# Prompt attention of a decoder step: turning of weights three units behind the scores in place of two

## The chip, the cores and the metric

One Trainium2 chip, one of its cores. The metric is the device time of one execution in microseconds (us). The kernel is written by hand for each engine: TensorE (PE, its weight loads PEld), VectorE (DVE), ScalarE (ACT), GpSimd (POOL) and SyncE (SP, which only starts DMAs), each with its own queue of instructions that it works off in order, and semaphores between them.

## What is computed

One step of a one-layer hybrid decoder: a prompt of 1024 tokens and 64 sample tokens, model width 1024. RMSNorm, one projection into queries, keys and values of 16 heads of width 64, attention, RMSNorm, output projection, residual, RMSNorm, an MLP with squared ReLU, final RMSNorm. Eight heads use stick-breaking attention, eight use dilated window attention with a softmax. For the prompt, cut to what matters here:

```python
# stick-breaking, strictly causal
z = q @ k.T * d**-0.5 + sb_bias[h]
log_1m = where(mask, log_sigmoid(-z), 0.0)
excl = cumsum(log_1m, reverse=True) - log_1m
o = where(mask, exp(log_sigmoid(z) + excl), 0.0) @ v
# dilated: the three patterns (128,1), (512,4), (2048,16), mixed by their softmax denominators
logits = q @ k.T * d**-0.5 + rel_bias[bucket(distance)]
```

The kernel joins the three dilated patterns to one softmax over all keys: a table by distance holds the bias plus the logarithm of how many patterns take that distance.

## The kernel before, in words

The stages run one after another: first norm, projection with sample attention, a stage that writes keys and values in natural order, **prompt attention** (prompt_stage, L924), output projection (dense_stage), MLP, store. Only prompt_stage is touched by the diff.

prompt_stage works through NU = 64 units. A unit is one pair of heads (two heads at once, 64 rows of TensorE each), one kind (stick-breaking, SB, or dilated, DIL) and one block of 128 queries. Query block q needs q + 1 blocks of 128 keys. For each of the four pairs come eight SB units and then eight DIL units. The list `order` (L933) takes the query blocks as 0, 7, 1, 6, 2, 5, 3, 4, so that the units of each eight are 1, 8, 2, 7, 3, 6, 4, 5 key blocks wide. In this document A0 to A7 are the eight SB units of a pair in this order, D0 to D7 its eight DIL units; so A1 and D1 have eight blocks, A3 and D3 seven. Light units (1, 2, 3, 4 blocks) have one piece, heavy ones (8, 7, 6, 5) have two: a piece is at most PW = 512 keys, four blocks. Light and heavy units alternate.

What is done for a unit:

- score (L1060, on PE): q times k for both heads into s_ps, two slots of one piece each; for SB the last block also gets a causal mask (L1081). It waits until the piece two before has been read out (L1072).
- SB: gate (L1130, ACT): two sigmoids per head and piece, into take (L1145) and stay (L1147). stay has two slots, so the gates of an SB unit wait for the product of the SB unit two before (L1134). Then broken (L1190, DVE): a reverse running product over stay for each head (L1197), times take in place (L1201).
- DIL: dilated (L1203, DVE): scale and bias for each piece into take (L1215), then the row minimum (L1221). Then exponent (L1151, ACT): exp over the unit, once per head, in place in take (L1157).
- turn (L1084, PE): 128 by 128 transposes of take into t_ps (L1095). t_ps has two slots of one piece of one head. So a unit with two pieces fills both slots with its first piece (head 0, head 1), and the second piece waits until ACT has copied them (L1093).
- copy_out (L1160, ACT): t_ps into wtsT (L1169), in SBUF.
- values (L1098, PE): v times the turned weights into o_ps (L1107), for DIL also ones times the weights for the softmax sum (L1112). It waits for o_out of the unit two before.
- o_out (L1223, DVE): a copy for SB (L1230), a reciprocal and a product for DIL (L1235, L1237), into o_T. SP stores o_T once eight units of a kind are done (L1042).

Each engine has one loop over a step s, and the order in it is the order of its queue. On PE (L1116): score(s) piece 0, turn(s-2) piece 0, score(s) piece 1, turn(s-2) piece 1, values(s-3). On ACT (L1172): gate(s) piece 0, copy_out(s-2) piece 0, gate(s) piece 1, copy_out(s-2) piece 1, and last exponent(s). On DVE (L1239): dilated(s), broken(s-1), o_out(s-4). The step is named by the unit that is scored in it, so that "step D3" is the one that scores D3.

take has WS = 4 slots of one unit (both heads, 1024 keys). Whoever writes a slot (gate L1136, dilated L1211) waits until the unit that held it, s-4, has been turned.

Of the rest, POOL turns the DIL queries around, once a pair (L1053), and SP loads q, k and v of the pair after next (L1008).

Of the kernel before, what the change touches and what calls it, by code (L numbers as in the profile page):

```python
# [382 lines left out]
def dense_stage(nc, cx, tag, weights, src, gain, ones, groups, hi, lo, turns, load=None, store=None, residual=None, keep=None,  # L383
# [10 lines left out]

    PW = 256
    per = KC // groups
    with ExitStack() as st:
# [16 lines left out]
        with nc.Block() as block:  # L414
            @block.sync
            def _(sp):
                def fetch(i, s):
                    col = i * 2 * PW + s * PW
                    col = col if isinstance(i, int) else sp.snap(col)
# [504 lines left out]
def prompt_stage(nc, cx, qkvT, oT, by_distance, sb_bias, neg_causal, ident, ones, v_nat):  # L924
# [3 lines left out]

    SB, DIL = 0, 1
    NU = 2 * PAIRS * QT  # L930
    WS = 4
    PW = 512
    order = [q for i in range(QT // 2) for q in (i, QT - 1 - i)]  # L933

    def unit(s):
# [3 lines left out]
    def kind(s):  # L939
        return s // QT % 2  # L940

    def width(s):
        return (unit(s)[2] + 1) * P

    def pieces(s):
        return [(a, min(PW, width(s) - a)) for a in range(0, width(s), PW)]

# [18 lines left out]
    with ExitStack() as st:  # L966
# [7 lines left out]
        stay = sb("stay", [P, 2, 2, SEQ])  # L974
        take = sb("take", [P, WS, 2, SEQ])
        prod = sb("prod", [P, 2, SEQ + 1])
# [29 lines left out]
        with nc.Block() as block:  # L1006
# [49 lines left out]
            @block.tensor  # L1056
            def _(pe):
                pe.wait_ge(tables_ready, 4)

                def score(s, some):  # L1060
                    j, k, q = unit(s)
                    if s % QT == 0:
                        pe.wait_ge(qk_loaded[k][j % 2], 32 * (j // 2 + 1))
                        if k == DIL:
                            pe.wait_ge(q_turned, j + 1)
                    for p, (a, n) in enumerate(pieces(s)):
                        if p not in some:
                            continue
                        g = piece[s, p]
                        if g >= 2:  # L1070
                            k2, count = scores_read[g - 2]
                            pe.wait_ge((gates, logits)[k2], count)  # L1072
                        masked = k == SB and a + n == width(s)
                        for h in range(2):
                            rows, cols = slice(h * HD, (h + 1) * HD), slice(q * P, (q + 1) * P)
                            queries = q_back[rows, j % 2, cols] if k == DIL else q_in[rows, SB, j % 2, cols]
                            last = pe.matmul(s_ps[:, g % 2, h, 0:n], queries, k_in[rows, k, j % 2, a:a + n], start=True,
                                             stop=not masked)
                        if masked:
                            for h in range(2):  # L1080
                                last = pe.matmul(s_ps[:, g % 2, h, n - P:n], identb[:, :], maskb[:, :], start=False, stop=True)  # L1081
                        last.then_inc(scored, 1)

                def turn(s, some):  # L1084
                    j, k, q = unit(s)
                    pe.wait_ge((sb_weights, dil_weights)[k], (1, 2)[k] * (of_kind(s, k) + 1))
                    for p, (a, n) in enumerate(pieces(s)):
                        if p not in some:
                            continue
                        for h in range(2):  # L1090
                            g = turned_piece[s, p, h]
                            if g >= 2:
                                pe.wait_ge(copied, g - 1)  # L1093
                            for b in range(0, n, P):
                                last = pe.transpose(t_ps[:, g % 2, b:b + P], take[:, s % WS, h, a + b:a + b + P], ident[:, :])  # L1095
                            last.then_inc(turned, 1)

                def values(s):  # L1098
                    j, k, q = unit(s)
                    pe.wait_ge(copied, 2 * pieces_to(s + 1))  # L1100
                    if s >= 2:
                        pe.wait_ge(o_copied, s - 1)
                    if s % QT == 0:
                        pe.wait_ge(v_loaded[k][j % 2], 16 * (j // 2 + 1))
                    for c in range(q + 1):
                        for h in range(2):
                            last = pe.matmul(o_ps[h * HD:(h + 1) * HD, s % 2, 0:P], v_in[:, k, j % 2, c, h * HD:(h + 1) * HD],  # L1107
                                             wtsT[:, s % 2, h, c, :], start=(c == 0), stop=(c == q))
                    if k == DIL:
                        for c in range(q + 1):  # L1110
                            for h in range(2):
                                last = pe.matmul(o_ps[h * HD:(h + 1) * HD, s % 2, P:2 * P], ones[:, 0:HD],  # L1112
                                                 wtsT[:, s % 2, h, c, :], start=(c == 0), stop=(c == q))
                    last.then_inc(o_done, 1)

                for s in range(NU + 3):  # L1116

                    for p in range(2):
                        if s < NU:
                            score(s, [p])  # L1120
                        if 0 <= s - 2 < NU:
                            turn(s - 2, [p])
                    if 0 <= s - 3 < NU:
                        values(s - 3)

            @block.scalar
            def _(act):
                act.wait_ge(tables_ready, 4)

                def gate(s, some):  # L1130
                    j, k, q = unit(s)
                    w = of_kind(s, SB)
                    if w >= 2:
                        act.wait_ge(sb_weights, w - 1)  # L1134
                    if s >= WS:
                        act.wait_ge(turned, 2 * pieces_to(s - WS + 1))  # L1136
                    for p, (a, n) in enumerate(pieces(s)):
                        if p not in some:
                            continue
                        g = piece[s, p]  # L1140
                        act.wait_ge(scored, g + 1)
                        for h in range(2):
                            head = 2 * j + h
                            z = s_ps[:, g % 2, h, 0:n]
                            act.activation(take[:, s % WS, h, a:a + n], z, ACT.Sigmoid, scale=SCALE,  # L1145
                                           bias=zb[:, 0, head:head + 1])
                            last = act.activation(stay[:, w % 2, h, a:a + n], z, ACT.Sigmoid, scale=-SCALE,  # L1147
                                                  bias=zb[:, 1, head:head + 1])
                        last.then_inc(gates, 1)

                def exponent(s):  # L1151
                    r = of_kind(s, DIL)
                    act.wait_ge(topped, r + 1)
                    for h in range(2):

                        x = take[:, s % WS, h, 0:width(s)]
                        act.activation(x, x, ACT.Exp, bias=top[:, r % 2, h:h + 1], scale=-1.0)\  # L1157
                           .then_inc(dil_weights, 1)

                def copy_out(s, some):  # L1160
                    if s >= 2:
                        act.wait_ge(o_done, s - 1)
                    for p, (a, n) in enumerate(pieces(s)):
                        if p not in some:
                            continue
                        for h in range(2):
                            g = turned_piece[s, p, h]
                            act.wait_ge(turned, g + 1)
                            act.activation(wtsT[:, s % 2, h, a // P:(a + n) // P, :], t_ps[:, g % 2, 0:n].rearrange(  # L1169
                                "p (c q) -> p c q", q=P), ACT.Copy).then_inc(copied, 1)  # L1170

                for s in range(NU + 3):  # L1172
                    for p in range(2):
                        if s < NU and kind(s) == SB:
                            gate(s, [p])
                        if 0 <= s - 2 < NU:
                            copy_out(s - 2, [p])
                    if s < NU and kind(s) == DIL:
                        exponent(s)

            @block.vector
            def _(dve):
# [53 lines left out]
                    dve.wait_ge(inverted, r + 1)  # L1236
                    dve.tensor_tensor(out, o[:, ::-1], one_over[:, ::-1], ALU.mult).then_inc(o_copied, 1)  # L1237

                for s in range(NU + 4):  # L1239
                    if s < NU and kind(s) == DIL:  # L1240
                        dilated(s)
                    if 0 <= s - 1 < NU and kind(s - 1) == SB:
                        broken(s - 1)
                    if 0 <= s - 4 < NU:
                        o_out(s - 4)


def projection_and_sample_stage(nc, cx, w_in, hi, lo, root, qkvT, oT, sb_bias, sb_caches, win_caches, q_back, new_rows, neg_new,
# [786 lines left out]
```

## Time and profile before

| | |
|---|---|
| median of 3 runs | 2104.06 us (2103.48 to 2105.66) |
| the profiled execution | 2106.2 us, its span 2104.4 us |
| PE busy | 1795.7 us, 85% of the span |
| DVE busy | 941.0 us, 45% |
| ACT busy | 560.9 us, 27% |
| POOL busy | 522.3 us, 25% |
| mean granted TensorE clock | 0.928 of full speed |

The span is from the first to the last instruction in the profile of one execution. Prompt attention lies between about 797 and 1141 us of it. Times in rows are us from the start of the span, durations in us.

### The profile page before, as it was taken

The page shows a single profiled execution, that of the slowest core. Times are in us where ns is not written, and L with a number is a line of the kernel's source. Part 1 is how long each engine was busy: PE and PEld are TensorE (multiplying, and loading weights), DVE is VectorE, ACT ScalarE, POOL GpSimd, SP SyncE. Part 2 cuts the span into 40 slices and gives each one's busy share as a digit, 9 for nine tenths or more (in the row PEclk, how much of TensorE's full clock was granted, in tenths as well). Part 3 has the DMA queues.
Part 4 walks back from the last instruction along what each step waited for, and adds up shares of the span by engine and source line. Part 5 has one row for each costly group of instructions (what it writes and reads, how often), then busy time and mean ns, then how long its engine had stood idle before and what let it go on. Part 6 is the DMA issues. An engine that isn't in the chain of part 4 may idle for free. (4 is left out here: it accounts for less than half of the span.)

```text
span 2104.4 us, 39226 instructions
## 1 busy us (share of the span) xinstructions
PE 1795.7 (85%) x17442; PEld 1554.3 (74%) x17442; DVE 941.0 (45%) x858; ACT 560.9 (27%) x927; POOL 522.3 (25%) x391
## 2 busy tenths in 40 slices
PE   6659579988789955978976696999999999999997
PEld 4447467766667743655644696999999999999997
DVE  2237347747457225787875847312121222122123
ACT  2202112202122115666664303202121111112022
POOL 0133436654466400000001113111122211122210
PEclk7889789998799967999998798999999999999999
DMA  7758779988799785121002403243333434333422
GB/s 208 262 201 335 268 275 390 414 351 325 279 343 414 278 320 202 41 81 41 12 11 113 158 1 127 93 167 123 131 119 119 157 122 139 119 119 119 160 99 95
DMA packets 112774, 385.74 MB, mean 183 GB/s; under 512 B 15064, under 2 KB 44248, under 8 KB 100568
## 3 DMA queue, kind: packets, MB, share of 16 engines
q0 software_dynamic: 39936, 251.41, 31.8%
q1 hardware_dynamic: 65912, 129.77, 17.6%
q10 hardware_dynamic: 6800, 2.68, 0.6%
q8 instruction: 102, 1.67, 0.3%
q14 instruction: 24, 0.20, 0.0%
HBM read 348.64 MB, written 102.04 MB: 214 GB/s over the span
## 5 line engine op out<-in xcount | busy, mean ns | idle before, releaser
L637 POOL TENSOR_TENSOR mlp_w_lo<-mlp_raw,mlp_w_hi 128x2048 fp32r<-128x2048 f32 x30 | 138.1, 4604 | 586.0 <-ACT mlp_w_hi L683 586.0
L1789 DVE STREAM_TRANSPOSE sa_kT<-sa_k_in 128x2048 f32<-128x2048 f32 x64 | 144.2, 2290 | 141.3 <-PE sa_s L1518 140.8
L796 DVE TENSOR_TENSOR xT<-xT,mlp_acc 128x1088 f32<-128x1088 f32 x64 | 82.5, 1289 | 278.7 <-PE mlp_acc L378 278.7
L378 PE MATMUL mlp_acc<-n_hi,mlp_w_hi 128*128 128x272 f32 x1024 | 171.8, 290 | 21.2 <-POOL mlp_w_lo L354 16.3
L1509 PE MATMUL sa_acc<-n_hi,sa_wh 128*128 128x512 f32 x384 | 158.5, 413 | 22.2 <-POOL sa_wl L1444 22.2
L378 PE MATMUL mlp_acc<-mlp_h_hi,mlp_w_hi 128*128 128x272 f32 x1024 | 170.4, 288 | 4.0 <-DVE mlp_h_lo L792 4.0
L378 PE MATMUL mlp_acc<-n_lo,mlp_w_hi 128*128 128x272 f32 x1024 | 170.7, 289 | 0.0
L378 PE MATMUL mlp_acc<-n_hi,mlp_w_lo 128*128 128x272 f32 x1024 | 170.5, 289 | 0.0
L378 PE MATMUL mlp_acc<-mlp_h_lo,mlp_w_hi 128*128 128x272 f32 x1024 | 169.6, 288 | 0.0
L378 PE MATMUL mlp_acc<-mlp_h_hi,mlp_w_lo 128*128 128x272 f32 x1024 | 169.6, 287 | 0.0
L378 PEld LDWEIGHTS mlp_acc<-n_hi,mlp_w_hi 128*128 128x128 f32 x1024 | 145.3, 190 | 22.5 <-POOL mlp_w_lo L354 16.5
L1595 PE MATMUL sa_o<-sa_v_in,sa_wtsT 128*16 128x128 f32 x2688 | 98.7, 290 | 65.9 <-DMA sa_v_in<-in_cache_win_v,sa_w_rows 32.7
L1509 PE MATMUL sa_acc<-n_lo,sa_wh 128*128 128x512 f32 x384 | 153.5, 400 | 0.0
L1509 PE MATMUL sa_acc<-n_hi,sa_wl 128*128 128x512 f32 x384 | 153.2, 399 | 0.0
L789 DVE SCALAR_TENSOR_TENSOR mlp_h<-mlp_acc,mlp_root 128x1088 f32<-128x1088 f32 x32 | 41.3, 1291 | 238.5 <-PE mlp_acc L378 238.1
L378 PEld LDWEIGHTS mlp_acc<-mlp_h_hi,mlp_w_hi 128*128 128x128 f32 x1024 | 143.6, 188 | 5.7 <-DVE mlp_h_lo L792 5.7
L378 PEld LDWEIGHTS mlp_acc<-n_lo,mlp_w_hi 128*128 128x128 f32 x1024 | 145.0, 189 | 0.0
L378 PEld LDWEIGHTS mlp_acc<-n_hi,mlp_w_lo 128*128 128x128 f32 x1024 | 144.7, 189 | 0.0
L378 PEld LDWEIGHTS mlp_acc<-mlp_h_lo,mlp_w_hi 128*128 128x128 f32 x1024 | 143.7, 188 | 0.0
L378 PEld LDWEIGHTS mlp_acc<-mlp_h_hi,mlp_w_lo 128*128 128x128 f32 x1024 | 143.7, 188 | 0.0
L1471 POOL DMA_INDIRECT sa_v_in<-in_cache_sb_v,v_rows x128 | 122.9, 960 | 76.4 <-PE sa_o L1595 51.6
L1595 PEld LDWEIGHTS sa_o<-sa_v_in,sa_wtsT 128*16 128x16 f32 x2688 | 68.1, 100 | 97.3 <-DMA sa_v_in<-in_cache_sb_v,v_rows 44.7
(180 smaller groups left out, 3006.5 us busy)
## 6 DMA issues: line engine op xcount, KB each, us to landing
out<-in_cache_win_k POOLq DMA_DIRECT2D x16, 2040.0 KB, 8.6
out<-in_cache_win_v POOLq DMA_DIRECT2D x16, 2040.0 KB, 8.6
mlp_raw<-in_w_up SPq DMA_DIRECT2D x16, 1024.0 KB, 11.7
mlp_raw<-in_w_down SPq DMA_DIRECT2D x16, 1024.0 KB, 11.3
fi_w<-in_w_in SPq DMA_DIRECT2D x24, 512.0 KB, 9.2
sa_wr<-in_w_in SPq DMA_DIRECT2D x24, 512.0 KB
qkvT<-sa_out SPq DMA_DIRECT2D x48, 256.0 KB, 5.5
na_rows_in<-qkvT SPq DMA_DIRECT2D x16, 512.0 KB, 7.0
```

What stands on the lines that cost most here:

```text
L378: last = pe.matmul(out[:, b, 0:BW], w[:, k, w_cols], x[:, k, b * BW:(b + 1) * BW], start=(k == 0 and part == 0), stop=(k == kn - 1 and par ...
L637: pool.tensor_tensor(out=ring.lo[:, n % 2, :], in0=ring.raw[:, n % 2, :], in1=ring.hi[:, n % 2, :].bitcast(F32), op=ALU.subtract).then_inc ...
L789: dve.scalar_tensor_tensor(out=in_banks(act_h[:, c % 2, :]), in0=acc[:, c % 2, :, 0:BW], scalar=0.0, in1=in_banks(root[:, :]), op0=ALU.max ...
L796: dve.tensor_tensor(in_banks(xT[:, c, :]), in_banks(xT[:, c, :]), acc[:, c % 2, :, 0:BW], ALU.add).then_inc(added, 1)
L1471: pool.indirect_dma_start(v_in[:, y % VS, :], None, src, bass.IndirectOffsetOnAxis(ap=rows, axis=0)).then_inc(v_loaded[y % VS], 16)
L1509: last_one = pe.matmul(acc[:, z % 3, :], w[:, k, :], x[:, k, cols], start=(k == 0 and part == 0), stop=(k == KC - 1 and part == 2))
L1595: last_one = pe.matmul(o_ps[c * 32:c * 32 + 2 * TS, a, :], w[:, a, c * 2 * TS:(c + 1) * 2 * TS], v[:, c * P:(c + 1) * P], start=False, sto ...
L1789: dve.transpose(kT[:, x % KT, :, :].rearrange("p x (j k) -> p j x k", k=32), k_in[:, x % KS, :, :].rearrange("p j (x d) -> p j x d", d=32) ...
```

## The change

Three constants or offsets change: the turning stands LAG = 3 steps behind the scores in place of 2, and with it copy_out, values and o_out one step later each; take has five slots in place of four. Gates, exponents, running products and their order among themselves stay as they are. take grows by 8 KB in each partition.

```diff
-    WS = 4
+    WS = 5
     PW = 512
+    LAG = 3
...
-                for s in range(NU + 3):
+                for s in range(NU + LAG + 1):
 
                     for p in range(2):
                         if s < NU:
                             score(s, [p])
-                        if 0 <= s - 2 < NU:
-                            turn(s - 2, [p])
-                    if 0 <= s - 3 < NU:
-                        values(s - 3)
+                        if 0 <= s - LAG < NU:
+                            turn(s - LAG, [p])
+                    if 0 <= s - LAG - 1 < NU:
+                        values(s - LAG - 1)
...
-                for s in range(NU + 3):
+                for s in range(NU + LAG + 1):
                     for p in range(2):
                         if s < NU and kind(s) == SB:
                             gate(s, [p])
-                        if 0 <= s - 2 < NU:
-                            copy_out(s - 2, [p])
+                        if 0 <= s - LAG < NU:
+                            copy_out(s - LAG, [p])
                     if s < NU and kind(s) == DIL:
                         exponent(s)
...
-                for s in range(NU + 4):
+                for s in range(NU + LAG + 2):
...
-                    if 0 <= s - 4 < NU:
-                        o_out(s - 4)
+                    if 0 <= s - LAG - 2 < NU:
+                        o_out(s - LAG - 2)
```

## Rows read from the trace of the kernel before

**Rows 1.** Windows: one A and one D stretch; busy us of PE, PEld, DVE, ACT, POOL.

```profile
966.30:1009.00 42.70, 33.54 (x300) 21.47 (x296) 32.90 (x33) 31.65 (x69) 1.13 (x1) 0.96 0.15 50
...
1009.00:1049.80 40.80, 38.00 (x394) 26.83 (x394) 32.12 (x37) 25.02 (x47) 0.00 (x0) 0.96 0.04 15
```

**Rows 2.** Timeline of DVE: running products of A6, the four pairs.

```profile
835.94 2.33 DVE L1197 TENSOR_TENSOR_SCAN pr_prod<-pr_stay 128x512 f32<-128x512 f32 x2
...
918.82 2.33 DVE L1197 TENSOR_TENSOR_SCAN pr_prod<-pr_stay 128x512 f32<-128x512 f32 x2
...
1002.85 2.33 DVE L1197 TENSOR_TENSOR_SCAN pr_prod<-pr_stay 128x512 f32<-128x512 f32 x2
...
1086.03 2.33 DVE L1197 TENSOR_TENSOR_SCAN pr_prod<-pr_stay 128x512 f32<-128x512 f32 x2
```

**Rows 3.** List of waits in the stage: us in total, times, longest us.

```profile
PE pr_turned L1095 <- DVE pr_take L1201: 28.1, 16, 5.3
```

**Rows 4.** Timeline of ACT and DVE, A stretch: gates, copies, running products.

```profile
815.16 1.10 ACT L1169 ACTIVATE pr_wtsT<-pr_turned 128x512 f32<-128x512 f32 x2
...
816.82 0.58 ACT L1145 ACTIVATE pr_take<-pr_scores,pr_zb 128x384 f32<-128x384 f32 x1 [0.55 <-PE pr_scores L1081]
...
818.84 3.94 DVE L1197 TENSOR_TENSOR_SCAN pr_prod<-pr_stay 128x896 f32<-128x896 f32 x2 [3.95 <-ACT pr_stay L1147]
...
821.49 0.73 ACT L1169 ACTIVATE pr_wtsT<-pr_turned 128x256 f32<-128x256 f32 x2
...
830.62 3.41 DVE L1197 TENSOR_TENSOR_SCAN pr_prod<-pr_stay 128x768 f32<-128x768 f32 x2 [2.02 <-ACT pr_stay L1147]
...
973.51 0.52 ACT L1169 ACTIVATE pr_wtsT<-pr_turned 128x128 f32<-128x128 f32 x2
...
984.37 0.58 ACT L1145 ACTIVATE pr_take<-pr_scores,pr_zb 128x384 f32<-128x384 f32 x1 [0.20 <-PE pr_scores L1081]
```

**Rows 5.** Timeline, third pair, from D0 to D3.

```profile
1008.21 0.42 DVE L1215 SCALAR_TENSOR_TENSOR pr_take<-pr_scores,pr_bias 128x256 f32<-128x256 f32 x1 [1.57 <-PE pr_scores L1077]
...
1009.00 2.86 DVE L1197 TENSOR_TENSOR_SCAN pr_prod<-pr_stay 128x640 f32<-128x640 f32 x2
...
1017.38 2.29 DVE L1221 TENSOR_REDUCE pr_top<-pr_take 128x2 f32<-128x2048 f32 x1
...
1019.70 2.19 ACT L1157 ACTIVATE pr_take<-pr_take,pr_top 128x1024 f32<-128x1024 f32 x2 [2.67 <-DVE pr_top L1221]
...
1022.50 1.22 DVE L1215 SCALAR_TENSOR_TENSOR pr_take<-pr_scores,pr_bias 128x1024 f32<-128x1024 f32 x1 [1.12 <-PE pr_scores L1077]
```

**Rows 6.** Timeline of PE, ACT and DVE, third pair, from step D6 to the fourth A1.

```profile
1037.95 1.75 PE L1107 MATMUL pr_o<-pr_wtsT,pr_v_in 128*64 128x128 f32 x28 [0.17 <-DVE pr_o_T L1237]
...
1045.19 0.82 PE L1112 MATMUL pr_o<-pr_wtsT,ones 128*64 128x128 f32 x12
...
1045.76 1.55 ACT L1157 ACTIVATE pr_take<-pr_take,pr_top 128x640 f32<-128x640 f32 x2 [0.79 <-DVE pr_top L1221]
...
1045.94 0.49 PE L1077 MATMUL pr_scores<-pr_k_in,pr_q_in 64*128 64x128 f32 x4
...
1051.49 0.69 ACT L1145 ACTIVATE pr_take<-pr_scores,pr_zb 128x512 f32<-128x512 f32 x1 [0.76 <-PE pr_scores L1077]
...
1057.23 4.47 DVE L1197 TENSOR_TENSOR_SCAN pr_prod<-pr_stay 128x1024 f32<-128x1024 f32 x2 [5.04 <-ACT pr_stay L1147]
```

**Rows 7.** TensorE after two idle gaps of like length, and a window.

```profile
896.87 1.09 PE L1095 MATMUL pr_turned<-ident,pr_take 128*128 128x128 f32 x8 [2.45 <-DVE pr_take L1201]
...
980.58 1.76 PE L1095 MATMUL pr_turned<-ident,pr_take 128*128 128x128 f32 x8 [2.45 <-DVE pr_take L1201]
...
981.00:985.00 4.00, 4.00 (x21) 2.54 (x19) 3.93 (x6) 3.80 (x8) 1.13 (x1) 0.59 0.51 162
```

**Rows 8.** Timeline of DVE, end of the stage.

```profile
1126.04 1.22 DVE L1215 SCALAR_TENSOR_TENSOR pr_take<-pr_scores,pr_bias 128x1024 f32<-128x1024 f32 x1 [1.02 <-PE pr_scores L1077]
...
1140.83 0.29 DVE L1237 TENSOR_TENSOR pr_o_T<-pr_o,pr_one_over 128x128 f32<-128x128 f32 x1
```

Columns of Rows 1, and of the last line of Rows 7: stretch, its length, busy us and instructions of PE, PEld, DVE, ACT and POOL, granted TensorE clock as a share of full speed, DMA share, GB/s. Columns of a timeline: start, duration of the merged instructions, engine, line, operation, output and inputs, shapes, count; in brackets the idle time of the engine before them and who ended it.

## The prediction

> **What bounds it now.** I read the windows by stretch first, then the timeline of the three engines over one whole pair, and the list of waits of the stage. Prompt attention takes some 344 us of the span of 2104.4; everything outside is the same code. In an A stretch no engine is full: of 42.70 us PE works 33.54, DVE 32.90, ACT 31.65; in a D stretch PE works 38.00 of 40.80 [rows 1]. So an A stretch is set by waits from engine to engine, and a D stretch nearly by PE's queue. The pairs repeat: from the running product of one A6 to the next it is 82.9, 84.0 and 83.2 us [rows 2], mean 83.4. The ring in an A stretch is stay, which has two slots and keeps them: product of A1, gates of A3, running product of A3, product of A3, gates of A5. PE waits in it too, 28.1 us over the stage for products that it is to turn [rows 3]; that wait the change takes away, but ACT and DVE stand in the ring without it. The fifth slot of take loosens nothing there. It only keeps the old slack: a slot has to be free one unit later, and is turned one step later.
>
> The point to see is the parity. Heavy and light units alternate, so two behind pairs heavy with heavy (score of A3 with turn of A1), three behind pairs heavy with light (score of A3 with turn of A0). That evens out PE's and ACT's work by step, and it takes something away: with LAG 2 a second piece of score stands between the two pieces of a heavy turn; with LAG 3 the two pieces follow each other, and the second needs ACT's copies of the first (t_ps has two slots).
>
> **Terms.** I carried each wait forward over one pair, with durations of equal shapes, and compare the marks with the rows.
>
> (a) A stretches, a gain. ACT's order for A3 is gates of piece 0, a copy, gates of piece 1. The copy was four blocks (1.10 us) and then 0.55 us of waiting for scores in the first pair, 0.20 in the third; it becomes one block (0.52), the scores long there [rows 4]. A3's running product starts 1.2 to 1.3 us earlier in the first pair; in later pairs, where the second wait is shorter, some 0.8. For A5 the copy of four blocks (1.10) becomes one of two (0.73) [rows 4], 0.5 with the short wait behind it. DVE, which has A2 and A4 to finish meanwhile, is free just before. First pair: -1.8 us; later ones -1.3 each.
>
> (b) D0 to D3, a gain that is lost again. Before, DVE waits 1.57 us for D0's score, which stands behind a held-up turn of A5 and the values of A4 [rows 5]. With LAG 3 PE has a light turn in step A7 and scores D0 as soon as A7's first gates are out. Third pair: the running product of A7 moves from 1009.00 to 1007.5, and, as both scores of D1 are then ready, the minimum of D1 from 1017.38 to 1014.5: 2.9 us ahead. But in step D2 PE must turn A7, whose second piece waits for ACT's copies of the first. ACT has them in its step D2, behind exponent(D1), which needs that minimum (2.29) and takes 2.1: until 1018.9. PE, done with the first piece at 1015.45, stands until 1019.5, four us; then come the rest of the turn and the values of A6 (1.0), and the first score of D3 starts at 1021.3. DVE reads it at 1022.45, against 1022.50 [rows 5]. Gain: nothing. This wait is new; behind it in PE's queue are values(A6) and score(D3), and DVE, with D2 done, waits for that.
>
> (c) D4 to D7. The same once more: turn(D1)'s second piece waits for copies behind exponent(D3), PE standing from 1026.5 to 1029.4; in D6 only 0.3. PE reaches A0 at 1046.6, against 1045.94; exponent(D7), which hangs on DVE, starts at 1045.5, against 1045.76 [rows 6]: -0.3. PE arrives a little late although it has the turn of D5 and the values of D4 still ahead.
>
> (d) D to A, a loss. In step A0 PE now turns D5, two pieces. The copies of the first stand behind exponent(D7), the table load and the gates of A0, until 1050.0 and 1050.6. Then come the second piece (to 1050.9) and the values of D4 (twelve matmuls for the sum 0.82 [rows 6], the values themselves as many, 1.5 together), and only then the first score of A1 (1.1). Its gates start at 1053.5, against 1051.49, and ACT's own work until the running product of A1 is unchanged, 5.74: 1059.3, against 1057.23 [rows 6]: 2.1 later, 2.3 counted from exponent(D7).
>
> (e) One pair, from A6 to A6: -0.3 + 2.3 - 1.3 = +0.7. Three times: +2.1. The last D stretch: -0.5 (its D0 waits longer than in the third pair).
>
> (f) The tail. When the last D7 is scored, PE has the turn of D4 (0.8) and the values of D3 (28 matmuls at 1.75 and as many for ones [rows 6], 3.3) still to do which it had behind it before. Nothing of later units hides them. From D7's first read-out to the last o_out it was 15.1 us [rows 8]; I get 19.1: +4.0. The next stage waits for this store, so it passes whole.
>
> (g) Without cost: SP's stores and loads stand a step later, but the loads run a whole pair ahead (tens of us); POOL waits for scores alone. Semaphores and instructions are the same in number. Were that cover gone, a store would count only at the end, where it counts now.
>
> Sum at the clock as it was: -1.8 + 2.1 - 0.5 + 4.0 = +3.8 us.
>
> (h) The clock. After 2.45 us of idle PE the eight transposes took 1.76 us at 980.58 and the stretch behind them had a granted clock of 0.59, mostly the lower level of 1.2 GHz; after the same 2.45 us at 896.87 they took 1.09, at 2.4 GHz [rows 7]. So a gap of that length is followed by the lower level sometimes. The new gaps of (b) and (c) are 4.1 and 2.9 us, eight in all, and behind each stands work on the path (values, then a score). Below: no new fall, 0. Above: all eight, each 1.4 us (0.7 for the eight transposes as in the row, and, an estimate, as much again for the score behind them, which takes about as long), 11. I take 4, three of eight, since one of the two gaps in the rows was followed by it. The Trainium skill, "TensorE: Matmul & The Clock Gate", section "HAM oscillation — how this bites in real kernels", says that a gap which recurs in every iteration can let the clock fall in each, so that every burst starts slow; by it the sum would go to its upper bound. The rows agree only in part: the same gap was once followed by a fall and once not.
>
> **Sum:** +3.8 + 4 = +8. The sum is made against one execution (2106.2 us, span 2104.4, 2.1 above the median); against the median: 2104.06 + 8 = 2112.
>
> **Rivals.** A measurement of this kernel can tell about 0.2%, 4.2 us.
> - The clock does not change: +3.8, 2107.9. For: the clock was at 0.96 of full speed in both stretches, with idle gaps in them [rows 1], and total idle PE time hardly grows. Against: the gaps are longer. 0.22.
> - Nothing net: waits are absorbed in slack, tail and start cancel apart from 2 us: 2104 to 2106. For: errors of 0.3 us in each of some ten marks could do it. 0.11. With it belongs that the change does not do what it says, because turning never waits for its weights in that step; against it stands the wait for products [rows 3].
> - Faster: the lead of (b) is kept. It decides in step D2: if PE comes to D3's first score before 1018.5 in place of 1021.3. Then each pair keeps 2.9: per pair +0.7 - 2.9 = -2.2, three times -6.6; start -1.8; last D stretch -0.5 - 2.9; tail +4.0: -7.8, 2096.3. For: DVE does get ahead. Against: ACT's queue has the copies behind exponent(D1), in order. 0.07.
> - Worse: all gaps are followed by the lower level, and gaps in the A stretches (PE in steps A4 and A6, some 2.8 us each) too: +3.8 + 11 + 2 = +17, 2121. 0.10.
>
> **Numbers.** Forecast (2108.3 to 2117): 0.50. Slower by over 0.2%: 0.50 + 0.10 + a fifth of the first rival, 0.05 = 0.65. Within: 0.17 + 0.11 = 0.28. Faster: 0.07. The range takes in the second rival's upper half and most of the worse one: 2105 to 2119. The likeliest case's own range is 2108 to 2117.
>
> **What would show it.** In the third pair, counted from A6's running product: D1's minimum near +11.6 (was 14.5), D3's first read-out near +19.6 (was 19.65), the running product of A1 near +56.5 (was 54.4), the next A6 near +84. Waits of PE's turn (L1095) for ACT's copy (L1169) should grow to some 15 us a pair, and those for products [rows 3] nearly go. Tail: 19 us from D7's read-out to the last o_out. Wrong if a pair takes under 83 us, or if PE does not stand in steps D2 and A0; if the pair takes 84 but the granted clock in the D stretches stays at 0.96 or more, (h) is wrong.

## The result and the profile after

The changed kernel takes 2133.07 us (median of 4, 2129.26 to 2134.84), the kernel before 2103.77 (median of 4): ratio 1.0138, 95% interval 1.0118 to 1.0159, so 25 to 33 us slower. The forecast was slower by 8, with a range to 2119. The profiled execution took 2129.26 us. The page of it opens:

```profile
span 2127.4 us, 39219 instructions
...
PE 1808.6 (85%) x17442; PEld 1559.2 (73%) x17442; DVE 939.2 (44%) x858; ACT 563.8 (27%) x927; POOL 524.4 (25%) x391
```

All of it lies in prompt attention. Its windows, as in [rows 1] (columns: stretch, length, busy us of PE, PEld, DVE, ACT, POOL, granted clock, DMA share, GB/s), here a D and an A stretch of the third pair and then the stage as a whole:

```profile
1016.00:1062.00 46.00, 38.79 (x370) 26.43 (x367) 31.28 (x35) 25.06 (x49) 0.00 (x0) 0.93 0.03 13
...
1062.00:1107.00 45.00, 35.51 (x345) 24.01 (x342) 32.67 (x34) 33.03 (x69) 0.00 (x0) 0.96 0.03 13
...
799.00:1164.00 365.00, 296.79 (x2746) 197.80 (x2742) 257.40 (x271) 228.12 (x453) 7.90 (x4) 0.91 0.14 49
```

The same for the stage of the kernel before:

```profile
800.00:1141.00 341.00, 284.51 (x2746) 193.14 (x2742) 259.41 (x272) 224.87 (x453) 5.46 (x4) 0.96 0.15 53
```

The work did not grow: DVE and ACT are busy as before. PE is busy 12 us longer with the same 2746 recorded matmuls, at a granted clock of 0.91 in place of 0.96; the other half of the 24 us is idle time. The running products of A6, the marks of [rows 2]:

```profile
833.69 2.33 DVE L1198 TENSOR_TENSOR_SCAN pr_prod<-pr_stay 128x512 f32<-128x512 f32 x2
...
922.64 2.33 DVE L1198 TENSOR_TENSOR_SCAN pr_prod<-pr_stay 128x512 f32<-128x512 f32 x2
...
1012.02 2.33 DVE L1198 TENSOR_TENSOR_SCAN pr_prod<-pr_stay 128x512 f32<-128x512 f32 x2
...
1103.42 2.33 DVE L1198 TENSOR_TENSOR_SCAN pr_prod<-pr_stay 128x512 f32<-128x512 f32 x2
```

A pair takes 89.0, 89.4 and 91.4 us, mean 89.9; it was 83.4, and +0.7 was forecast, before the clock. From the last A6 to the end of the stage it is longer too. The first load of the next stage, on SP's queue, after and before:

```profile
1167.46 0.38 SPq L423 DMA_DIRECT2D out_raw<-in_w_out  x1
```

```profile
1144.24 0.38 SPq L423 DMA_DIRECT2D out_raw<-in_w_out  x1
```

From the last A6 to this load it is 64.0 us, against 58.2. The list of waits of the stage (total us, times, longest); PE's wait for products [rows 3] is gone, and in its place stand these:

```profile
PE pr_turned L1096 <- ACT pr_wtsT L1170: 56.5, 32, 3.7
...
DVE pr_take L1216 <- PE pr_scores L1078: 53.7, 23, 6.1
```

Steps D2 to D4 of the third pair, on the timeline:

```profile
1027.90 2.19 ACT L1158 ACTIVATE pr_take<-pr_take,pr_top 128x1024 f32<-128x1024 f32 x2 [4.26 <-DVE pr_top L1222]
...
1029.99 1.76 ACT L1170 ACTIVATE pr_wtsT<-pr_turned 128x512 f32<-128x512 f32 x4
...
1030.71 0.73 PE L1096 MATMUL pr_turned<-ident,pr_take 128*128 128x128 f32 x2 [3.64 <-ACT pr_wtsT L1170]
...
1032.77 2.08 PE L1078 MATMUL pr_scores<-pr_k_in,pr_q_back 64*128 64x512 f32 x4
...
1034.96 1.22 DVE L1216 SCALAR_TENSOR_TENSOR pr_take<-pr_scores,pr_bias 128x1024 f32<-128x1024 f32 x1 [5.45 <-PE pr_scores L1078]
...
1042.07 1.85 PE L1096 MATMUL pr_turned<-ident,pr_take 128*128 128x128 f32 x8 [2.64 <-ACT pr_wtsT L1170]
...
1044.90 1.45 PE L1078 MATMUL pr_scores<-pr_k_in,pr_q_back 64*128 64x512 f32 x4
...
1046.47 1.84 DVE L1216 SCALAR_TENSOR_TENSOR pr_take<-pr_scores,pr_bias 128x1024 f32<-128x1024 f32 x2 [4.85 <-PE pr_scores L1078]
```

This is the chain of the forecast. ACT's exponent of D1 (1027.90, 2.19 us) stands ahead of its copies (1029.99). PE has turned the first piece of A7 and waits 3.64 us for the slots. But then the first score piece of D3 (four matmuls of 512 keys) takes 2.08 us and not 1.13, and DVE has waited 5.45 us for it; [rows 5] has 1.12 there. Two steps later once more: transposes 1.85, score 1.45, DVE 4.85 us idle. In this pair the same stands at two more places, which have no price in the forecast's sum. First the gap of step A6, and D0's read-out that it holds back:

```profile
1009.97 0.94 PE L1096 MATMUL pr_turned<-ident,pr_take 128*128 128x128 f32 x6 [2.29 <-ACT pr_wtsT L1170]
...
1011.43 2.08 PE L1078 MATMUL pr_scores<-pr_k_in,pr_q_in 64*128 64x512 f32 x4
...
1017.84 0.42 DVE L1216 SCALAR_TENSOR_TENSOR pr_take<-pr_scores,pr_bias 128x256 f32<-128x256 f32 x1 [2.02 <-PE pr_scores L1078]
```

Then step A0, up to the running product of A1:

```profile
1064.97 0.83 PE L1096 MATMUL pr_turned<-ident,pr_take 128*128 128x128 f32 x4 [2.29 <-ACT pr_wtsT L1170]
...
1068.21 1.74 PE L1078 MATMUL pr_scores<-pr_k_in,pr_q_in 64*128 64x512 f32 x4
...
1070.38 0.69 ACT L1146 ACTIVATE pr_take<-pr_scores,pr_zb 128x512 f32<-128x512 f32 x1 [4.15 <-PE pr_scores L1078]
...
1076.11 4.47 DVE L1198 TENSOR_TENSOR_SCAN pr_prod<-pr_stay 128x1024 f32<-128x1024 f32 x2 [6.51 <-ACT pr_stay L1148]
```

And the granted clock of the stretches behind the gaps of D2, of A0 and of A6:

```profile
1030.70:1035.00 4.30, 4.20 (x23) 2.06 (x24) 0.04 (x1) 1.69 (x5) 0.00 (x0) 0.64 0.00 0
...
1064.00:1070.50 6.50, 5.53 (x38) 3.68 (x39) 2.42 (x5) 2.16 (x7) 0.00 (x0) 0.74 0.00 0
...
1011.30:1015.00 3.70, 3.70 (x16) 1.74 (x12) 3.67 (x5) 1.54 (x4) 0.00 (x0) 0.54 0.00 0
```

A score piece of 2.08 us is at the lower level (1.2 GHz), one of 1.13 at 2.4 GHz; one between is partly at the lower, and all above 1.13 are called slow here. Over the four pairs the score behind the gap of D2 (3.64 to 3.67 us idle) was slow each time, 1.55 to 2.08 us, and that behind the gap of D4 (2.64) three times, 1.45 to 2.08. Behind the gaps of A6 (2.29 to 2.57) and A0 (2.29) it was slow in the third pair alone and took 1.13 in the others. The third pair, shown here, is the longest for that reason.

### The profile page after: what moved, and what is told of

It is laid out like the page before. It is cut to its first block and busy times, and to the rows that moved or that the text cites. A ratio compares the mean times of both kernels' runs of the same rounds, so it can differ in the third digit from the quotient of the medians.

```text
span 2127.4 us, 39219 instructions
## 1 busy us (share of the span) xinstructions
PE 1808.6 (85%) x17442; PEld 1559.2 (73%) x17442; DVE 939.2 (44%) x858; ACT 563.8 (27%) x927; POOL 524.4 (25%) x391
## 5 line engine op out<-in xcount | busy, mean ns | idle before, releaser
L1096 PEld LDWEIGHTS pr_turned<-ident,pr_take 128*128 128x128 f32 x576 | 65.6, 147 | 105.7 <-issue 77.9
```

## The experiments

All were timed beside the kernel before on the same chip; its medians there were 2106.5 to 2106.7 us, so kernels are compared by their ratios. Times are medians, ratios against the kernel before with 95% intervals. LAG = 3 unless something else is said. Marks of the third pair, in us from A6's running product: the minimum of D1, D3, D5 and D7, the running product of A1, and the next A6.

| kernel | us | ratio | D1 | D3 | D5 | D7 | A1 | A6 |
|---|---|---|---|---|---|---|---|---|
| before | 2103.8 | 1 | 14.5 | 22.5 | 32.0 | 41.4 | 54.4 | 83.2 |
| changed | 2133.1 | 1.0138 | 13.5 | 25.3 | 36.3 | 46.4 | 64.1 | 91.4 |
| extra matmuls in five gaps | 2117.5 | 1.0052 | 11.9 | 22.1 | 31.5 | 41.7 | 57.7 | 85.0 |
| extra matmuls in three gaps | 2122.9 | 1.0083 | 11.9 | 23.7 | 33.1 | 43.2 | 59.3 | 86.6 |
| LAG 4 | 2104.5 | 0.9996 | 14.9 | 23.1 | 30.2 | 39.4 | 52.4 | 81.7 |
| late exponent | 2094.4 | 0.9936 | 11.9 | 19.0 | 26.6 | 36.7 | 51.8 | 79.1 |
| late exponent, scores together | 2088.0 | 0.9919 | 11.8 | 18.8 | 25.8 | 35.8 | 50.6 | 77.9 |

My theory was the one of the forecast: at distance three the second piece of a heavy turn waits for copies that ACT has behind the exponent of a heavy unit, and the gap brings the lower clock. The rivals were the fifth slot, the distance itself, and either half of the theory alone.

**1. The fifth slot alone.**

```diff
-    LAG = 3
+    LAG = 2
```

> LAG back to 2, five slots of take kept. Theory (the lost time is in the pairing of heavy turns with light scores): as the kernel before, 2104 us within 4. Rival (the fifth slot itself costs, by its place in SBUF or its waits): a good part of the 29 us stays, 2115 or more.

Measured: 2105.7 us, ratio 0.9998 (0.9982 to 1.0015). The slot alone costs nothing; the rival falls.

**2. One step further.**

```diff
-    WS = 5
+    WS = 6
-    LAG = 3
+    LAG = 4
```

> LAG = 4 and six slots of take, so heavy turns stand beside heavy scores again. Theory of parity: the waits of the second piece for ACT's copies are gone again; the pair is back at 83 to 84.5 us, and only the tail grows (by the turn of D3 and the values of D2 on top of what LAG 3 added): 2104 to 2112 us. Rival (distance itself costs): one step more costs as much again, 2150 us or more.

Measured: 2104.5 us, ratio 0.9996 (0.9979 to 1.0014). Distance as such is not what costs, which leaves parity. Pairs take 83.0, 82.1 and 81.7 us, less than before; the tail gives that back (last A6 to the next stage's load 63.0 us, before 58.2). Its window of the stage, the scores of the DIL units (min, median, max ns) here and in the changed kernel, and a score of D0 here:

```profile
798.00:1139.00 341.00, 293.77 (x2744) 199.89 (x2742) 258.59 (x272) 224.39 (x451) 4.16 (x4) 0.91 0.15 52
```

```profile
L1078 PE MATMUL pr_scores<-pr_k_in,pr_q_back x192: 272/588/693, 838.5 to 1116.8; 64*128 64x512 f32 x96, 64*128 64x128 f32 x32, 64*128 64x256 f32 x32, 64*128 64x384 f32 x32
```

```profile
L1078 PE MATMUL pr_scores<-pr_k_in,pr_q_back x192: 272/589/1220, 837.2 to 1145.8; 64*128 64x512 f32 x96, 64*128 64x128 f32 x32, 64*128 64x256 f32 x32, 64*128 64x384 f32 x32
```

```profile
1002.82 0.80 PE L1078 MATMUL pr_scores<-pr_k_in,pr_q_back 64*128 64x128 f32 x4
```

The granted clock of the stage is 0.91, as low as in the changed kernel, and yet the pairs are on the mean shorter than before (82.3 against 83.4 us). No DIL score of 512 keys runs at the lower level here (longest 693 ns); in the changed kernel 22 of 96 do (up to 1220). Here the lower level falls on work of the A stretches and of the step of D0, its short scores among it: 0.80 us for four matmuls of 128 keys, where [rows 6] has 0.49. So the mean clock alone says little; it matters which instructions it hits. That the ones it hits here have slack is read from the pairs' length and was not tested by itself.

**3. The exponent out of the way of the copies.** On ACT:

```diff
-                        if s < NU and kind(s) == SB:
+                        late = p == 0 and 0 <= s - 1 < NU and kind(s - 1) == DIL
+                        if s < NU and kind(s) == SB and not late:
                             gate(s, [p])
                         if 0 <= s - LAG < NU:
                             copy_out(s - LAG, [p])
-                    if s < NU and kind(s) == DIL:
-                        exponent(s)
+                        if late:
+                            exponent(s - 1)
+                        if s < NU and kind(s) == SB and late:
+                            gate(s, [p])
```

In the step behind D7 the gates of A0 thus stand behind a copy and the exponent too.

> LAG = 3, but ACT does exponent(s-1) after the copy of the first piece of step s, in place of exponent(s) at the end of step s. Theory: PE no longer stands in steps D2, D4 and A0 for copies behind an exponent, and with these gaps the lower clock behind them goes: a pair falls from 89.3 us to 84 or less, the whole to 2100 to 2112. Rival (the lower clock or the A stretch are what costs, the waits in the D stretches not): 2122 or more.

Measured: 2094.4 us, ratio 0.9936 (0.9910 to 0.9961): faster than expected, and faster than the kernel before. Step D2 of the third pair:

```profile
1007.30 1.09 ACT L1170 ACTIVATE pr_wtsT<-pr_turned 128x512 f32<-128x512 f32 x2 [1.10 <-PE pr_turned L1096]
...
1008.04 0.73 PE L1096 MATMUL pr_turned<-ident,pr_take 128*128 128x128 f32 x2 [0.42 <-ACT pr_wtsT L1170]
...
1008.39 2.19 ACT L1158 ACTIVATE pr_take<-pr_take,pr_top 128x1024 f32<-128x1024 f32 x2
...
1009.72 1.13 PE L1078 MATMUL pr_scores<-pr_k_in,pr_q_back 64*128 64x512 f32 x4
```

The copies (1007.30) now stand ahead of the exponent (1008.39), PE waits 0.42 us where it waited 3.64, and the score of D3 takes 1.13. The lead of 2.9 us that the forecast saw as gained and lost again is kept: D3 stands at 19.0 us, before at 22.5. The gap of step A6 is still there. Behind it the score is slow in the second and fourth pair, and just there D1 stands at 13.4 and 13.5 us, in the others at 11.8 and 11.9.

**4. The gaps filled, no wait taken away.** In turn, ahead of the wait for the slots (L1093):

```diff
+                        nxt = s + LAG + 1
+                        if p == 1 and nxt < NU and (k, s % QT) in ((SB, 7), (DIL, 1), (DIL, 5), (SB, 1), (SB, 3)):
+                            g = piece[nxt, 0]
+                            k2, count = scores_read[g - 2]
+                            pe.wait_ge((gates, logits)[k2], count)
+                            for _ in range(32):
+                                pe.matmul(s_ps[:, g % 2, 0, 0:P], identb[:, :], maskb[:, :], start=True, stop=True)
```

The 32 matmuls write, with no use for the result, into the slot of the next score, once its last read-out is over.

> The changed kernel with 32 extra bfloat16 matmuls of 128 columns (about 2 us, their result unused) on PE between the two pieces of the turns of A7, D1, D5, A1 and A3, where it stands anyway. They add work and take no wait away. Theory (the lower clock after the gaps makes up the larger part of the loss): scores and values after the gaps take 1.1 us in place of 1.5 to 2.1, and the time falls by 8 to 18 us, to 2115 to 2125. Rival (waits alone): no gain, 2133 or up to 6 us more.

Measured: 2117.5 us, ratio 1.0052 (1.0034 to 1.0071), some 16 to 18 us less than the changed kernel, with more work on PE. Step D2 of the third pair, PE, and the same score in the fourth pair:

```profile
1016.16 1.95 PE L1097 MATMUL pr_scores<-pr_maskb,pr_identb 128*128 128x128 bf16 x32
...
1019.87 0.33 PE L1103 MATMUL pr_turned<-ident,pr_take 128*128 128x128 f32 x1 [1.76 <-ACT pr_wtsT L1177]
...
1021.64 1.13 PE L1078 MATMUL pr_scores<-pr_k_in,pr_q_back 64*128 64x512 f32 x4
...
1107.66 1.58 PE L1078 MATMUL pr_scores<-pr_k_in,pr_q_back 64*128 64x512 f32 x4
```

The 32 matmuls stand in the gap; what is left of the wait is 1.76 us, and the first score of D3 takes 1.13. It is so in two of the four pairs. In the first and fourth this score is slow even so (1.74 and 1.58 us), and D3 follows D1 there some 1.5 us later than in the other two. The window of the stage:

```profile
799.00:1149.00 350.00, 312.83 (x3350) 224.39 (x3346) 257.26 (x272) 227.18 (x451) 6.20 (x3) 0.97 0.14 50
```

Clock 0.97. From the first product of the stage (the negated bias, zb, on DVE) to the next stage's first load it is 356.5 us, 14 less than in the changed kernel (370.6). Set against the changed kernel the marks of the third pair differ by 1.6 us in D1, 1.6 more in D3, 1.6 more in D5, nothing more in D7, 1.6 more in A1 and nothing after: four falls of the clock, those seen in the rows of the result, at 1.6 us each.

**5. Only three of the gaps filled.** As in 4, with the list cut to (SB, 7), (DIL, 1), (DIL, 5).

> The changed kernel with the extra matmuls only in the turns of A7, D1 and D5, that is in the gaps of steps D2, D4 and A0, not in those of A4 and A6. Theory (the clock matters where PE is nearly full, in the D stretches and at the step from D to A): most of what the five gaps gave is kept, 2117 to 2123 us. Rival (the gaps of the A stretches matter as much): 2126 or more.

Measured: 2122.9 us, ratio 1.0083 (1.0059 to 1.0106), at the upper end. Of the 0.86% that five filled gaps gave, these three keep 0.55. The other 0.31 would be the worth of the two in the A stretches, more than I thought, but the intervals of 4 and 5 overlap. The marks say where it acts. Of this kernel's four pairs two have D1 at 11.8 and 11.9 us, two at 13.8 and 13.5, and with all five filled it is 11.8 to 12.2 in each. And behind the filled gap of D2 the score is slow in three pairs here, in two with all five filled.

**6. Two pieces of a turn together, LAG = 2.** On PE:

```diff
-                    for p in range(2):
-                        if s < NU:
-                            score(s, [p])
-                        if 0 <= s - LAG < NU:
-                            turn(s - LAG, [p])
+                    if s < NU:
+                        score(s, [0, 1])
+                    if 0 <= s - LAG < NU:
+                        turn(s - LAG, [0, 1])
```

> LAG = 2 with PE's order score both pieces, then turn both pieces: the pieces of a heavy turn follow each other as they do with LAG 3, but the exponent ahead of ACT's copies is still that of a light unit. Theory (it costs only because the copies stand behind the exponent of a heavy unit): 2100 to 2112 us. Rival (two pieces of a turn behind each other are enough to cost it, whatever ACT does): 2120 or more.

Measured: 2100.8 us, ratio 0.9979 (0.9965 to 0.9993). Two pieces behind each other do not bring the loss. They are not free of waits: over the stage PE waits 33.3 us for copies, before 17.8, though never more than 2.1 at a time. The edit also scores both pieces of a heavy unit at once, which by the medians gives 6 us at LAG 3 (9 against 3), so a small cost of the turns may be hidden by it. Together with 3, what costs is what ACT has ahead of the copies.

**7. The late exponent with LAG = 2.** The edit of 3.

> LAG = 2 with ACT's late exponent, the order that helped with LAG 3. Theory: with LAG 2 there is little to remove (PE idles 2.8 us in a D stretch), so 2098 to 2107 us, and the gain of the late exponent is one of LAG 3. Rival (the late exponent helps by itself): 2095 or less, as with LAG 3.

Measured: 2109.4 us, ratio 1.0013 (0.9999 to 1.0028), just above what was expected. No gain: the late exponent helps at LAG 3, where it stood in the way of copies behind a heavy unit, and not by itself.

**8. Values into the gap, two misses and a hit.** On PE, first in every step:

```diff
                         if 0 <= s - LAG < NU:
                             turn(s - LAG, [p])
-                    if 0 <= s - LAG - 1 < NU:
-                        values(s - LAG - 1)
+                        if p == 0 and 0 <= s - LAG - 1 < NU:
+                            values(s - LAG - 1)
```

> LAG = 3, but PE does values(s-4) between the two pieces of turn(s-3), where it stands for ACT's copies. Theory: in steps D2, D4 and A0 the wait covers 1.0, 0.6 and 1.5 us of values that had stood behind it, so a pair loses at least 3 us less, and more where the shorter gap is not followed by the lower clock: 2112 to 2124 us. Rival (the waits are not on the path): 2130 or more.

Measured: 2181.4 us, ratio 1.0363 (1.0341 to 1.0385). And together with the late exponent:

> LAG = 3 with the late exponent and values between the two pieces of a turn. Theory: what PE still waits for copies (33 us over the stage with the late exponent alone) is partly filled with values: 2084 to 2092 us. Rival (these waits are in A stretches, where PE has slack): 2094 within 3.

Measured: 2141.2 us, ratio 1.0166 (1.0136 to 1.0196). Both missed by far. I had looked at the steps with a heavy turn only. In the others the values now stand between the two pieces of a heavy score, and the waits of the first of the two say so (total us, times, longest):

```profile
ACT pr_take L1158 <- DVE pr_top L1222: 93.5, 16, 6.7
...
PE pr_o L1108 <- DVE pr_o_T L1238: 33.7, 13, 3.9
```

DVE's minimum comes late, and ACT waits 93.5 us for it (50.4 in the changed kernel); and PE itself waits 33.7 us for o_out, since it asks for the o_ps slot earlier in the step; in the changed kernel it is some 4 us. The mended edit moves values only where a heavy turn stands beside a light score:

```diff
+                        between = s - LAG < NU and len(pieces(max(s - LAG, 0))) == 2 and (s >= NU or len(pieces(s)) == 1)
+                        if p == (0 if between else 1) and 0 <= s - LAG - 1 < NU:
+                            values(s - LAG - 1)
```

> LAG = 3; values(s-4) between the two pieces of turn(s-3) only where a heavy turn stands beside a light score; elsewhere at the end of the step as in the changed kernel. Theory (the earlier run lost because values stood in front of the second score of a heavy unit and in front of its own o_ps): the waits for copies are partly covered and the lower clock comes less: 2112 to 2128 us. Rival (values in the gap always costs, by the wait for o_out): above 2133.

Measured: 2108.9 us, ratio 1.0011 (0.9997 to 1.0025), better than expected. With the gaps filled by work that was due anyway, nearly all of the loss is gone. Some scores are still slow behind them (2.08 us in the first pair); how much of the gain is the clock and how much the shorter path was not taken apart.

**9. The fastest.** The late exponent of 3 and the order of PE of 6, with LAG = 3.

> LAG = 3 with the late exponent, and PE scores both pieces of a heavy unit before the light turn. Theory: the second piece comes 0.25 to 1.0 us earlier to DVE or ACT in each heavy unit: 2086 to 2094 us. Rival (that piece is not what they wait for): 2094 within 3.

Measured: 2088.0 us, ratio 0.9919 (0.9895 to 0.9943). And with the extra matmuls in the turns of A1 and A3:

> The fastest kernel so far (LAG = 3, late exponent, scores together, 2088 us) with the 32 extra matmuls in the turns of A1 and A3, the gaps of steps A4 and A6. Theory (the lower clock after the gap of step A6 holds back D0's score, which is why D1's minimum comes 13.2 us after A6's running product in three pairs of four and 11.5 in the other): D1 at 11.5 to 11.8 in all four pairs, 2083 to 2087 us. Rival (the 1.6 us have another cause, or the extra matmuls cost what they give): 2088 within 2.

Measured: 2083.8 us, ratio 0.9890 (0.9872 to 0.9908). The intervals of the two overlap, but the marks show the effect: D1 stands at 11.4, 11.8, 11.8 and 11.8 us in the four pairs, where it stood at 11.5, 13.2, 11.8 and 13.1 (the forecast of three at 13.2 had taken one pair too many). Both beat the kernel before, by 0.8 and 1.1%.

## Why the prediction was wrong

**The sign and the mechanism of the waits held.** Parity (2), the copies behind a heavy exponent (3, 6, 7), PE standing in steps D2, D4 and A0, and the free fifth slot (1) came as forecast.

**(a) to (f), the terms at an unchanged clock, +3.8.** The kernel with the filled gaps is the test, since it keeps the waits. Its third pair has D1 at 11.9 (11.6 forecast), A1 at 57.7 (56.5) and A6 at 85.0 (84). The gain at the start of the stage, from zb's product to the first A6, was 1.3 us in the changed kernel (1.8 forecast); from D7's minimum to the next stage's load it lost 4.5 (4.0 forecast). The parts of a pair that no fall touches, put together over the four pairs (D1 at 11.8 to 11.9, then 10.3, 9.4, 10.1, 15.7 to 16.0 and 27.3 us), come to 84.7, so +1.3 a pair where I had +0.7. The last D stretch came out at -0.2 (-0.5 forecast). In all: -1.3 + 3.9 - 0.2 + 4.5 = +6.9. Undersized by 3 us, by errors of some tenths at each mark.

**(h), the clock, is the step that failed.** I took 4 us and at most 11; the runs show about 17. In the changed kernel's own profile the marks above these parts come to 17 us: 7.4 in front of D3 (all four pairs), 6.0 in front of D5 (three of four), 1.9 in front of D1 (of which 0.3, in the second pair, stands with filled gaps too) and 1.6 in front of A1. With 6.9 that is 24, the 24.2 us by which the stage grew (from zb's product to the next load, 370.6 against 346.4). Three things were wrong in it. First the number: I took three of eight gaps, because one of two like gaps before had been followed by a fall (one of two would even be four of eight), and seven of eight were. The trace of the kernel before has a third gap of 2.45 us, also without a fall:

```profile
1064.08 1.09 PE L1095 MATMUL pr_turned<-ident,pr_take 128*128 128x128 f32 x8 [2.45 <-DVE pr_take L1201]
```

So one of three was the record of an A stretch, and it did not carry over to the longer gaps of the D stretches. Second the price: 1.4 for one fall was close (1.6 as a rule), but two cost 2.8. Third the places: I counted only the gaps of D2 and D4. That of A0 is described in (d) and has no price at all, and those of A4 and A6 have one, 2 us, in the last rival alone.

The kernel with filled gaps settles that this is the clock and not more waiting: work was added, no wait taken away, and 14 of the 17 us went from the stage (16 to 18 from the time). The 3 that stayed are its two slow scores of D3. Why a gap is followed by a fall in one pair and not in the next stays open.

What the Trainium skill says in "TensorE: Matmul & The Clock Gate", section "HAM oscillation — how this bites in real kernels", and what I had weighed, is that a gap that recurs can let the clock fall each time. The changed kernel's D2 and D4 steps bear it out, seven of eight; its A6 and A0 steps (two of seven) and the gaps of 2.45 us in the kernel before (one of three) do so only in part. With LAG 4 the mean clock was as low, but never on a wide DIL score, and the pairs lost nothing.

The rest, from the 23 us between the two profiled executions to the 29 between the medians, is not explained by these profiles: the changed kernel's profiled run was its fastest of four, and the kernel before's lay 2 us above its median. That the others had more falls is likely and not shown.

**The rivals.** "Worse" had the right mechanism at 2121 us and a chance of 0.10; it was the case nearest to what came, and it was priced too low as well, since it too rests on the price of (h) and leaves out A0 and the falls that cost 2.8. "Faster: the lead of (b) is kept" did not come, but its condition was named rightly: with copies ahead of the exponent the lead is kept (3).

## What to carry to other kernels

Before changing the distance between stages of a software pipeline whose units alternate in size, write down which pairs of units then share a step, on every engine's queue: here the same edit costs 1.4% at distance three, nothing at four, and gains 0.6% at three once ACT's copies go ahead of its exponent (0.8% with PE's scores of a unit together). A new gap on TensorE that recurs should be priced as the gap plus a fall of the clock, wherever the work behind it is on the path: here gaps of 2.64 to 3.67 us were followed by one seven times of eight, gaps of 2.29 to 2.57 two times of seven, and a fall cost 1.6 us, sometimes 2.8. Such a gap can be filled with work that is due anyway, but only in the steps that have the gap.

## What was not expected of the hardware

Two kernels with the same mean granted clock in the stage, 0.91, differed by 1.4% in time. In the slower one the lower level fell on scores on the path, wide DIL ones above all; by the marks that is 17 us of the 24 by which its stage is longer. In the other it fell elsewhere. And 32 matmuls without use in a gap of 3.6 us, some 2 us of work, were followed by a score at the upper level in two of four pairs, where without them all four were slow, and in the gap of D4 in four of four, where three had been slow: adding work to a waiting engine took 16 us off the time.
